# Two transformer blocks on one core: turned blocks moved from SBUF to SBUF on SyncE's queue instead of over DRAM on ScalarE's

## The reference

```python
D_FF = -(-8 * D_MODEL // (3 * 256)) * 256       # 5632
h2 = _rmsnorm(x, ffn_norm_w[l])
g, u = jnp.split(jnp.einsum('bsd,df->bsf', h2, w_gate_up[l]), 2, axis=-1)
x = x + jnp.einsum('bsf,fd->bsd', jax.nn.silu(g) * u, w_down[l])
```

## Time and profile before

| | before |
|---|---|
| median of 3 runs | 2449.92 us |
| the profiled execution | 2450.19 us |
| its span, first to last instruction | 2448.2 us |
| TensorE busy | 2440.5 us |
| VectorE busy | 1765.0 us |
| ScalarE busy | 1189.3 us |
| granted clock | 1.000 (2.4 GHz) |
| HBM read, written | 587.80 MB, 11.55 MB |

### The profile page before, as it was taken

How to read it: one execution, slowest core, us unless ns; L and a number is a source line. 1 busy time by engine, 2 the same in 40 slices (tenths; PEclk the granted TensorE clock), 3 DMA queues, 4 the chain that set the end, 5 groups by cost and what they waited for, 6 DMA issues and landing times.

```text
span 2448.2 us, 29306 instructions
## 1 busy us (share of the span) xinstructions
PE 2440.5 (100%) x11700; PEld 2140.9 (87%) x11700; DVE 1765.0 (72%) x2216; ACT 1189.3 (49%) x1451; POOL 26.0 (1%) x27
## 2 busy tenths in 40 slices
PE   9999999999999999999999999999999999999999
PEld 8898888888888888888888888888888888888888
DVE  7787797777788778786666566796778775556555
ACT  6444545544444444445765554444644443444443
POOL 0000000000000000000010000000000000000000
PEclk9999999999999999999999999999999999999999
DMA  8656656688888878886455446887488986566754
GB/s 304 235 195 233 231 207 243 245 305 298 299 292 297 306 278 299 295 294 218 175 188 174 155 172 240 303 292 247 174 293 301 312 289 204 200 220 230 230 200 149
DMA packets 108087, 601.25 MB, mean 246 GB/s; under 512 B 11440, under 2 KB 30256, under 8 KB 38320
## 3 DMA queue, kind: packets, MB, share of 16 engines
q1 hardware_dynamic: 83040, 580.39, 67.2%
q10 hardware_dynamic: 24912, 19.00, 2.7%
HBM read 587.80 MB, written 11.55 MB: 245 GB/s over the span
## 4 chain that ended last, share of the span: by engine, by line
PE 99%; DMA 0%; DVE 0%; ACT 0%; SPq 0%; issue 0%; POOL 0%; ACTq 0%
PE bank L883 32%; PE bank L884 31%; PE bank L885 31%; PE bank L593 2%; PE bank L673 1%; PE bank L711 0%; DMA raw<-in_w_in_dram 0%; PE bank L722 0%; PE bank L723 0%; PE bank L692 0%; PE bank L681 0%; PE bank L691 0%; PE bank L712 0%; PE bank L734 0%; PE bank L866 0%; PE bank L867 0%
## 5 line engine op out<-in xcount | busy, mean ns | idle before, releaser
L1335 DVE TENSOR_TENSOR wlo<-raw,whi 128x1024 fp32r<-128x1024 f32 x885 | 1079.0, 1222 | 595.6 <-ACT whi L920 591.8
L920 ACT CAST whi<-raw 128x1024 fp32r<-128x1024 f32 x885 | 927.0, 1049 | 954.9 <-PE bank L885 943.2
L883 PE MATMUL bank<-whi,hH 128*128 128x512 f32 x2528 | 968.5, 383 | 2.0 <-DVE wlo L1335 1.3
L884 PE MATMUL bank<-wlo,hH 128*128 128x512 f32 x2528 | 958.1, 379 | 0.0
L885 PE MATMUL bank<-whi,hL 128*128 128x512 f32 x2528 | 958.1, 379 | 0.0
L883 PEld LDWEIGHTS bank<-whi,hH 128*128 128x128 f32 x2528 | 477.9, 189 | 69.7 <-DVE wlo L1335 1.7
L885 PEld LDWEIGHTS bank<-whi,hL 128*128 128x128 f32 x2528 | 477.8, 189 | 67.9
L884 PEld LDWEIGHTS bank<-wlo,hH 128*128 128x128 f32 x2528 | 478.1, 189 | 65.4
L1814 DVE SCALAR_TENSOR_TENSOR adacc<-raw,stat,adacc 128x512 f32<-128x512 f32 x360 | 269.8, 749 | 6.8
L883 PE MATMUL bank<-whi,aH 128*128 128x512 f32 x704 | 267.4, 380 | 0.0
L884 PE MATMUL bank<-wlo,aH 128*128 128x512 f32 x704 | 266.8, 379 | 0.0
(11 more groups left out here) (308 smaller groups left out, 1410.9 us busy)
## 6 DMA issues: line engine op xcount, KB each, us to landing
raw<-in_w_gu_dram SPq DMA_DIRECT2D x176, 1024.0 KB, 5.2
raw<-in_w_ada_dram SPq DMA_DIRECT2D x96, 1024.0 KB, 4.9
raw<-in_w_down_dram SPq DMA_DIRECT2D x88, 1024.0 KB, 4.8
raw<-in_w_in_dram SPq DMA_DIRECT2D x60, 1024.0 KB, 4.8
raw<-in_w_in2b_dram SPq DMA_DIRECT2D x56, 1024.0 KB, 4.8
raw<-in_w_out_dram SPq DMA_DIRECT2D x32, 1024.0 KB, 4.8
across<-tmp ACTq DMA_DIRECT2D x36, 256.0 KB, 4.1
turned<-across ACTq DMA_DIRECT2D x72, 128.0 KB, 6.4
```

Of the source, the lines that this page charges most:

```text
L883: e.matmul(o, xh[:, kt, sl], pairs(wh, i), start=k == 0, stop=False)
L884: e.matmul(o, xh[:, kt, sl], pairs(wl, i), start=False, stop=False)
L920: e.copy(whi[i][:, :, :], raw[u % RAW][:, 2 * hf:2 * hf + 2, :]).then_inc(*ev("act_hi", c, 0))
L1335: e.tensor_tensor(wlo[i][:, :, :], raw[u % RAW][:, 2 * hf:2 * hf + 2, :], f(whi[i][:, :, :]), ALU.subtract).then_inc(*ev("dve_lo", c, 0))
```

## The change

The DRAM tensor and ScalarE's six transfers go. SyncE issues sixteen transfers instead, each from 32 partitions of `T` to 32 partitions of `FT` (2 x 128 columns, 32 KB, in pieces of 512 bytes). For that, `T[0]` to `T[3]` become halves of two tensors `T2` at the same addresses. They are issued ahead of the first unit whose buffer is released in slot last+3 or later. The cast moves from step 11 to step 8, the low half from step 12 to step 9.

```diff
-        T = [new(f"tmp{i}", [P, 512]) for i in range(7)]
+        T2 = [new(f"two{i}", [P, 2, 512]) for i in range(2)]
+        T = [t[:, m, :] for t in T2 for m in range(2)] + [new(f"tmp{i}", [P, 512]) for i in range(4, 7)]
...
-        across = nc.dram_tensor("across", (2, 2, P, 512), F32, kind="Internal").ap()
...
+        def moved(b):
+
+            return sem_moved, 256 * (ups.index(b) + 1)
...
-                elif kind == "fup" and t == 3 and b in ups:
-                    n = ups.index(b)
-                    if n >= 2:
-                        e.wait_ge(*landed(ups[n - 2]))
-                    for m in range(2):
-                        e.wait_ge(*on("dve_turned", b.index, m))
-                        e.dma_start(across[n % 2, m], ffn_tmp(b.arg[1], m)[:, :]).then_inc(sem_away, 16)
-                elif kind == "fup" and t == 6 and b in ups:
-                    e.wait_ge(*sent(b))
-                    rows = across[ups.index(b) % 2].rearrange("m (i p) (q c) -> q p m i c", i=4, q=4)
-                    for q in range(4):
-                        e.dma_start(FT[32 * q:32 * q + 32, :, :].rearrange("p m (i c) -> p m i c", i=4),
-                                    rows[q]).then_inc(sem_back, 16)
-                elif kind == "fup" and t == 11 and b in ups:
+                elif kind == "fup" and t == 8 and b in ups:
                     f_, j = b.arg
                     k0 = 4 * (j - PARTS[j >= 6][0])
-                    e.wait_ge(*landed(b))
+                    e.wait_ge(*moved(b))
...
-                elif kind == "fup" and t == 12 and b in ups:
+                elif kind == "fup" and t == 9 and b in ups:
...
+            def turn_over(u):
+
+                for b in ups:
+                    if u == after(pl.last[b.index, 1] + 3):
+                        for m in range(2):
+                            e.wait_ge(*on("dve_turned", b.index, m))
+                        for q in range(4):
+                            for i in range(4):
+                                e.dma_start(FT[32 * q:32 * q + 32, :, P * i:P * i + P],
+                                            T2[b.arg[1] % 2][32 * i:32 * i + 32, :, P * q:P * q + P]).then_inc(
+                                    sem_moved, 16)
+
...
                 gates(u)
+                turn_over(u)
```

More of the change, by code:

```diff
@@ L472, in two_block_kernel @@
         sem_row, sem_gt = sem("s_row"), sem("s_gt")
-        sem_away, sem_back = sem("s_away"), sem("s_back")
+        sem_moved = sem("s_moved")
         sem_ident, sem_fw, sem_am, sem_out = sem("s_ident"), sem("s_fw"), sem("s_am"), sem("s_out")
```

## The result

The changed kernel takes 2460.1 us (median of 5 runs, 2458.2 to 2460.82), the kernel before 2449.96 us: a ratio of 1.0040, 95% interval 1.0029 to 1.0051. That is 10 us slower. I had forecast 2449.9 us with a range up to 2456. By its time it is the rival "SyncE's issues become the bound", priced there at 2458 for 12 us of issue time, that came true.

The account below looks back on a forecast made before the run. The prediction took TensorE to bound the kernel, busy 2440.5 of 2448.2 us. Adding 0 for ScalarE and 0 for 18 turn-overs to 2450.19 us, it forecast a median of 2449.9 us, range 2449.0 to 2456.0.

Parts of the forecast that it names:

- SyncE's issues become the bound: Rival: slow issues on SyncE's queue delay loads until TensorE waits; 2458 us at 12 us, 2504 at 15.3; chance 0.12.
- The price of sixteen issues: On SyncE's queue, per tile: 7.4 to 7.8 us of issue time at 0.47 us each, costing TensorE 0.
- break-even of 9.4: In three tiles of block 1, TensorE waits only if sixteen issues exceed 9.4 us, 0.59 us per transfer.
- three signs of being wrong: Sixteen issues above 9.4 us; units behind landing over 10 us after issue; TensorE idle before L883 for `wlo`.
- upper bound, 15.3 us: Sixteen issues on SyncE's queue at 0.96 us each, from ScalarE's slowest four beside 1 MB units in flight.
- The sixteen at the start: Sixteen issues at the kernel's start, 256 to 512 KB each, that took 9.0 us; used as a comparison.
- the reading by which each is paid in turn: Rival: each transfer lands before the next moves, 86 us per tile, +1290 us, 3740 us; chance 0.01.
- formula x - 9.4: Loss in each of block 1's tiles j = 1, 4, 7 when sixteen issues take x us, above 9.4.
- Steps 8 and 9: Earlier cast on ScalarE and low half on VectorE; priced at 0, the casts fitting in ScalarE's idle time.
- worked tile: One block 1 tile with three close units, timed through: a load 1.8 us late, 2 us of cushion left.
- The removed path: ScalarE's six issues and the way over DRAM per tile; 9.4 MB less HBM traffic each way, gain 0.

Follow-up runs that it names:

- e4_forms: Changed kernel with its sixteen transfers in six forms in turn (DRAM or SBUF source, differing dimensions, pieces and partitions), three tiles each; 2459.1 us in a single execution.
- e3_half_data: Changed kernel with each of the sixteen transfers moving only half its data, 16 KB; 2459.0 us, ratio 1.0037.
- e5_from_dram: Changed kernel with the sixteen transfers read from a DRAM tensor instead of the SBUF temporaries; 2449.93 us, ratio 1.000.
- e6_from_dram_22: Changed kernel with the sixteen transfers read from DRAM and six more small DRAM transfers behind them; 2460.36 us, ratio 1.0043.
- e7_24_issues: Changed kernel with eight more small SBUF-to-SBUF transfers per tile, 24 in all; 2530.1 us, ratio 1.0328.
- e11_two_by_eight: Changed kernel with the sixteen issues in two groups of eight ahead of two successive units, steps 8 and 9 kept; 2450.29 us, ratio 1.0002.
- e2_late_cast: Changed kernel with only the cast moved back to step 11 and the low half to step 12; 2456.4 us, ratio 1.0027.
- e1_spread: Changed kernel with the sixteen issued four at a time ahead of four successive units, cast and low half at steps 11 and 12; 2450.0 us, ratio 1.000.
- e8_behind_three: Changed kernel with steps 11 and 12, and the sixteen put behind the three close units in three tiles of block 1; 2449.89 us, ratio 1.000.
- e10_gpsimd_queue: Changed kernel with the sixteen transfers issued by GpSimd instead of SyncE, cast and low half at steps 11 and 12; 2450.16 us, ratio 1.0001.
- e9_scalar_queue: Changed kernel with the sixteen transfers issued by ScalarE at step 3 instead of by SyncE; 2527.0 us, ratio 1.0317.

## Why the prediction was wrong

**What failed** is one term: "The price of sixteen issues", where I took 0.47 us per issue from `grow<-gT` and 7.4 to 7.8 us for sixteen. It measured 0.64 us and 10.2 to 11.4 us, above the break-even of 9.4, and with it two of the three signs of being wrong came: a row of sixteen over 9.4 us, and TensorE idle for a low half. The rows that I leaned on the earlier trace rows all have DRAM on one side, and e4_forms shows that of the properties tried there this is the one that counts: 0.47 with it, 0.64 without. I had treated the small size as what made the new transfers cheap ("a quarter of those"), and e3_half_data shows that size has no part in it. Only the upper bound, 15.3 us, held it. The sixteen at the start, 9.0 us with DRAM on one side, were closer than the figure I took, and show that 0.47 is not the price of every issue from DRAM either; I chose the low end as the nearest row.

**What held.** The mechanism: the time for which the queue is held, the place of the loss, and a break-even. The losses are in the three tiles where a `w_ada` unit and two weight units are released together: idle 1.24, 1.32 and 2.90 us. For j=1 the break-even was 9.4 us; there sixteen issues of 8.7 us cost nothing (e5_from_dram) and sixteen of 10.95 us cost 1.6 us, and the whole loss is the same whether they are SBUF transfers or others (e6_from_dram_22). The sixteen transfers overlap, as the prediction had it against the reading by which each is paid in turn. (The 2.0 us that it took from the Trainium skill is given there for transfers issued by GpSimd; these, issued by SyncE, landed in 1.9.) The one loss outside the three tiles, 1.07 us at j=4 of block 2, I did not foresee: there the late load is the last `w_ada` unit, and a matmul of the side work waits for its sum. That tile has the longest sixteen of all, 11.43 us.

**What was too low.** For j=1, with x = 10.95, the formula x - 9.4 gives 1.6 us, and start to start TensorE lost 1.6. At j=4 and j=7 the sixteen took 10.20 and 10.18 us, so the formula gives 0.8 each, and 1.7 and 3.2 were lost. I had worked one tile and taken its break-even for all three. At j=4 the sixteen began 12.4 us before the cast that came late was due, at j=1 and j=7 13.1 us before, so that tile has 0.7 us less to spare. At j=7 the 1.8 us of the table load and its neighbours stand in ScalarE's way between the late cast and the next, and the trace before had them in the same place. No run tests these two by themselves. In the profiled execution the gap at j=7 also drew a slower clock for 1.7 us more, which the rival's prices left out; in e7_24_issues the clock is what made it 80 and not 57.

**Steps 8 and 9**, counted at 0, are 0 with the loads in time (e11_two_by_eight) and 3.7 us with the loads late (the changed kernel against e2_late_cast; the loss in block 2 is there only with them). The prediction had these casts in the chain of its worked tile, but named no price for them where the cover is gone.

**The removed path** gave nothing, as forecast: HBM traffic fell by 9.4 MB each way, and TensorE had no gap to give back. A range to 2456 was too narrow for a threshold only 2 us above the estimate, when my own upper bound for sixteen issues reached 6 us beyond it; 0.12 was too little for that rival.

## What to carry to other kernels

A run of DMA issues on a queue costs its number times the time of one issue, and what pays is whatever stands behind it; price one issue from a row whose two sides lie in the same memories, since size and shape say little. Compare that product with the slack of the loads behind it, tile by tile, with all that stands in the way there, and where it is larger, break the run up between loads or put it behind the closest group of them: e1_spread and e8_behind_three cost nothing with the same sixteen transfers. An engine that nobody waits for can issue them as well (e10_gpsimd_queue), one whose work feeds TensorE can't issue sixteen in a row (e9_scalar_queue); in smaller groups that was not tried.

## What the runs showed of the hardware that was not expected

- An issue on SyncE's queue took 0.60 us from SBUF to SBUF and 0.43 us from DRAM to SBUF, in both cases with 0.04 us to the next, for 16 KB as for 32 KB (e3_half_data, e4_forms). From SBUF to SBUF GpSimd took 0.53 us, and ScalarE's queue 0.62.
- The Trainium skill (DMA: Bandwidth & Descriptors, Issuing engines are not separate DMA queues) says that what a sequencer spends on starting a DMA is usually small relative to the DMA itself. Here one issue took 0.60 us and its transfer landed after 1.9, about a third, and as the transfers overlap and the issues don't, sixteen issues took 10.2 us or more. For such a run the trace does not agree.
- A gap of some 2 us on TensorE can cost most of itself again in clock, but need not. The granted clock was 0.52 for 3.5 us behind the longest gap of the changed kernel (the second of two, some 3 us apart, 2.90 us idle in the two), and stayed at 1.00 at the three other places. At the same tile in e6_from_dram_22, with 2.58 us idle, and in e3_half_data, with 2.60, it stayed at 1.00 too. In e7_24_issues, with gaps in 14 tiles, it was 0.98 over 580 us and 0.96 over 230 us.
